# Router computed inside the merge's last products, with the normalisation applied to tokens on partitions

## The reference

```python
def merge_branches(gates, o_a, o_b, w_o_a, w_o_b, w_out):
    g_a, g_b = jnp.split(gates, 2, axis=-1)
    y = jax.nn.sigmoid(g_a) * (o_a @ w_o_a) + jax.nn.sigmoid(g_b) * (o_b @ w_o_b)
    return y @ w_out

def hier_moe(h, router_grp, router_grp_b, router_exp, router_exp_b, w_gate, w_up, w_down):
    t = h.reshape(-1, shape[-1])
    grp_p = jax.nn.softmax((t @ router_grp + router_grp_b).astype(jnp.float32), axis=-1)
    p_grp, g_sel = lax.top_k(grp_p, 1)                       # one of 4 groups
    exp_logits = (t @ router_exp + router_exp_b)...reshape(-1, N_GROUPS, EXPERTS_PER_GROUP)
    in_grp = jnp.take_along_axis(exp_logits, g_sel[:, :, None], axis=1)[:, 0]
    top_logit, top_idx = lax.top_k(in_grp, TOP_K)            # two of its 8 experts
    w_top = jax.nn.softmax(top_logit, axis=-1) * p_grp
    ...
        hid = silu(einsum('td,edf->tef', t, w_gate[grp])) * einsum('td,edf->tef', t, w_up[grp])
        out = out + einsum('tef,efd->td', hid * combine[:, grp, :, None], w_down[grp])

    h_lat = h_lat + m_lat[2] * y_lat
    h_lat = h_lat + m_lat[5] * hier_moe(
        modulate(rmsnorm(h_lat, norm_ffn_g[l]), m_lat[3], m_lat[4]), ...)
```

## Time and profile before

| | |
|---|---|
| median of 3 runs | 2619.45 us |
| profiled execution, its own time | 2621.55 us |
| its span | 2619.7 us |
| TensorE matmul busy | 2470.2 us (94%) |
| DVE busy | 1424.4 us (54%) |
| ACT busy | 1186.0 us (45%) |
| mean granted TensorE clock | 0.970 |
| chain that ended last, by engine | PE 75%, DVE 8%, issue 5%, DMA 5%, ACT 4% |

### The profile page before, as it was taken

The page is one execution under the profiler, slowest core; times in us unless marked ns, Lnnn a source line. Parts: engine busy times, 40 slices in busy tenths (PEclk is TensorE's granted clock), DMA queues, the critical chain, the costliest instruction groups (busy, mean ns, idle before and its releaser), DMA issues.

```text
span 2619.7 us, 52357 instructions
## 1 busy us (share of the span) xinstructions
PE 2470.2 (94%) x23199; PEld 2135.1 (82%) x23199; DVE 1424.4 (54%) x2229; ACT 1186.0 (45%) x1707; POOL 306.8 (12%) x425
## 2 busy tenths in 40 slices
PE   6999999999999999999999989899888889799998
PEld 6999888799999998878899965785477778678786
DVE  4654545466546645443666456445245540278885
ACT  4434466444444444564444355321254421167773
POOL 0100000021101100000311000641133321000000
PEclk8999999999999999999999989889899899899999
DMA  6754522256656644322566411101100004379993
GB/s 217 246 192 167 192 97 104 81 195 233 216 178 213 230 164 171 129 97 101 173 237 222 154 66 46 54 15 57 65 4 4 4 27 141 96 240 365 365 365 126
DMA packets 268884, 396.07 MB, mean 151 GB/s; under 512 B 9320, under 2 KB 172829, under 8 KB 268525
## 3 DMA queue, kind: packets, MB, share of 16 engines
q1 hardware_dynamic: 266921, 389.25, 43.4%
q0 software_dynamic: 1120, 2.17, 0.3%
q10 hardware_dynamic: 612, 1.24, 0.1%
HBM read 391.59 MB, written 1.05 MB: 150 GB/s over the span
## 4 chain that ended last, share of the span: by engine, by line
PE 75%; DVE 8%; issue 5%; DMA 5%; ACT 4%; POOL 2%; SPq 0%; ACTq 0%; DVEq 0%; POOLq 0%
PE ps L282 74%; DMA RB<-in_moe_w_up 5%; DVE gwl L431 2%; POOL H L1415 2%; ACT gwh L422 1%; POOL AR L2535 0%; ACT wh L422 0%; PE ps L1093 0%; DVE wl L431 0%; PE ps L520 0%; DVE AR L1677 0%; ACT AR L2752 0%; DMA RB<-in_ffn_w_gu 0%; ACT AR L2744 0%; DVE AT L1178 0%
## 5 line engine op out<-in xcount | busy, mean ns | idle before, releaser
L431 DVE TENSOR_TENSOR wl<-RB,wh 128x2048 fp32r<-128x2048 f32 (+4 forms) x188 | 412.5, 2197 | 294.5 <-ACT wh L422 293.9
L282 PE MATMUL ps<-H,RB 128*128 128x256 f32 (+1 forms) x1712 | 455.5, 423 | 1.1 <-ACT H L1515 1.1
L422 ACT ACTIVATE wh<-RB 128x2048 fp32r<-128x2048 f32 (+4 forms) x188 | 342.3, 1825 | 236.7 <-PE ps L282 205.3
L282 PEld LDWEIGHTS ps<-H,RB 128*128 128x128 f32 x1712 | 325.5, 193 | 115.1 <-issue 77.4
L282 PE MATMUL ps<-xhf,wl 128*128 128x256 f32 x1408 | 404.4, 287 | 14.0 <-DVE xlf L651 9.3
L282 PE MATMUL ps<-xlf,wh 128*128 128x256 f32 x1408 | 401.0, 285 | 0.0
L282 PE MATMUL ps<-xhf,wh 128*128 128x256 f32 x1408 | 400.8, 285 | 0.0
L282 PE MATMUL ps<-AR 64*64 64x64 f32 (+4 forms) x8296 | 276.1, 242 | 47.2 <-issue 19.7
L282 PEld LDWEIGHTS ps<-AR 64*64 64x64 f32 (+2 forms) x8296 | 241.9, 148 | 80.3 <-issue 51.0
L282 PEld LDWEIGHTS ps<-xhf,wl 128*128 128x128 f32 x1408 | 273.0, 194 | 24.9 <-DVE wl L431 14.8
L282 PEld LDWEIGHTS ps<-xlf,wh 128*128 128x128 f32 x1408 | 273.0, 194 | 0.1
(11 more groups left out here) (425 smaller groups left out, 4155.0 us busy)
## 6 DMA issues: line engine op xcount, KB each, us to landing
RB<-in_ffn_w_gu SPq DMA_DIRECT2D x88, 1024.0 KB, 7.7
RB<-in_w_in SPq DMA_DIRECT2D x25, 2048.0 KB, 7.7
RB<-in_ffn_w_down SPq DMA_DIRECT2D x16, 2048.0 KB, 7.8
RB<-in_w_gate SPq DMA_DIRECT2D x16, 2048.0 KB, 8.2
RB<-in_moe_w_gate SPq DMA_DIRECT2D x32, 1024.0 KB, 7.7
RB<-in_moe_w_up SPq DMA_DIRECT2D x32, 1024.0 KB, 10.2
RB<-in_moe_w_down SPq DMA_DIRECT2D x32, 1024.0 KB, 8.2
RB<-in_ada_w SPq DMA_DIRECT2D x12, 2048.0 KB, 9.9
```

The source lines that it names most:

```text
L282: return M.matmul(o, lhsT, rhs, start=start, stop=stop, skip_group_check=True)
L422: S.activation(self.pair(h)[0], of(slot_of(*key)), ACT.Copy).then_inc(*did("high", *mark))
L431: V.tensor_tensor(lo, of(slot_of(*key)), hi.bitcast(F32), ALU.subtract).then_inc(*did("low", *mark))
```

## The change

- The router's weights RTW are multiplied once by (1 + scale) of each feature, and the product of the shift with the unscaled RTW is added to the router's bias RTB. The 8 matmuls for that ("shifted") stand at the start of `merge` on TensorE; two small DVE instructions follow (L3004 and L3005 of the changed kernel).
- A new class `Route` holds the work on x. `Route.pe(c)` is issued behind the out2 product c + 1 and takes raw XT[c]: two transposes, two matmuls for the logits, and two matmuls that sum the squares (ACT, L3159) with tokens on partitions, so that the norm is one number per partition (1/rms, `rs`). The transposed rows get it as a scale when ACT copies them out, the logits in one DVE instruction each.
- The first two halves of expert weights are split within out2 (ACT behind tile 3 and 5, DVE the same); half 2 is split among the gathering as before.
- The group is chosen from the logits, by a scan, without the exponential. The `ranks` matmuls, the places, CHOSEN and the flag come directly behind it; the experts' choice and weights run on DVE while TensorE gathers.
- The gathering and its split are ahead of the branch. Scale and shift are applied to the gathered tokens: ACT writes X1 with scale and bias (L3204) and then copies it to xh (L3207); DVE subtracts from X1.
- out2 uses three PSUM banks, the logits bank 3, the transposed rows banks 4 to 7. The norm into HA is made in `dense` only.

```diff
@@ merge: tensor()
+                ps = bank(("shifted",), ("rt_bias",))
+                for k in range(KD):
+                    ins = mm(ps[:, 0:36], MOD[:, 24 + k, 0:1].broadcast_to([128, 128]), RTW[:, k, :], k == 0, k == KD - 1)
+                ins.then_inc(*did("shifted"))
                 branch_pe(0, OAT)
...
-                    ps = bank(("out2", c), ("mixed2", c))
+                    ps = bank(("out2", c), ("mixed2", c), among=(0, 1, 2))
...
+                    if c:
+                        route.pe(c - 1)
+                route.pe(KD - 1)
...
+            def pe(self, c):
+                if c == 0:
+                    self.ps = bank(("route",), ("logits", 1), among=(3,))
+                    PE.wait_ge(*at("rt_w"))
+                PE.wait_ge(*at("mixed2", c))
+                for t in LAT:
...
+                    ins = M.transpose(ps[:, 128 * (c % 4):128 * (c % 4) + 128], XT[:, c, 128 * t:128 * t + 128], ident)
...
+                for t in LAT:
+                    mm(self.ps[:, 36 * t:36 * t + 36], XT[:, c, 128 * t:128 * t + 128], RTW[:, c, :], c + t == 0, False)
+                PE.wait_ge(*at("squared", "n3", c))
+                for t in LAT:
+                    ins = mm(self.ps[:, 72 + 2 * t:74 + 2 * t], self.XS[:, c, 128 * t:128 * t + 128], ones[:, 0:2], False,
+                             c == KD - 1)
...
+            def act(self):
+                S.activation(self.ms, EPS, ACT.Sqrt).then_inc(*did("spread_root"))
                 for c in range(KD):
...
+                    AC.wait_ge(*at("mixed2", c))
+                    S.activation(self.XS[:, c, :], XT[:, c, :], ACT.Square).then_inc(*did("squared", "n3", c))
+                    if c in (3, 5):
+                        self.ws_g.high(c // 2)
...
+            def places_pe(self):
+                PE.wait_ge(*at("grouped"))
...
+                PE.wait_ge(*at("chosen"))
+                for k in range(KD):
...
+            def places_act(self):
...
+                    S.activation(self.X1[k % 2], ps_of("xm", k), ACT.Identity, bias=MOD[:, 24 + k, 0:1],
+                                 scale=SCL[:, 2, k:k + 1]).then_inc(*did("xm_out", k))
+                    AC.wait_ge(*at("xm_out", k))
+                    S.activation(self.xh[:, k, :], self.X1[k % 2], ACT.Copy).then_inc(*did("xm_high", k))
...
+        def experts(route):
+            route.places_pe()
+            route.places_act()
+            route.places_dve()
             for x in (PE, DV, AC, PO, SP):
                 x.wait_ge(*at("known"))
...
@@ gathered: tensor()
-                PE.wait_ge(*at("chosen"))
...
+                PE.wait_ge(*at("combined"))
                 ps = bank(("cw",), ("cw_out",), among=work)
```

More of the change, by code:

```diff
@@ new lines, in places_dve @@
+                ps = ps_of("ranks")
+                V.scalar_tensor_tensor(out=rank, in0=ps[:, 0:8].rearrange("p (t g) -> p t g", t=2), scalar=1.0, in1=sel,
+                                       op0=ALU.add, op1=ALU.mult).then_inc(*did("v"))
+                V.tensor_reduce(flag[:, 0:1], ps[:, 8:12], AXX, ALU.max).then_inc(*did("v"))
+                DV.wait_ge(*upto("v"))
+                V.tensor_scalar(rank, rank, -1.0, None, ALU.add).then_inc(*did("rank"))
+                V.tensor_scalar(flag[:, 1:2], flag[:, 0:1], 128.0, None, ALU.is_le).then_inc(*did("v"))
@@ new lines, in places_dve @@
+                DV.wait_ge(*at("rank"))
+                for t in range(2):
+                    for g in range(4):
+                        ins = V.tensor_scalar(self.CHOSEN[:, t, g, :], cst(C_NUM), rank[:, t, g:g + 1], None, ALU.is_equal)
+                ins.then_inc(*did("chosen"))
+                DV.wait_ge(*upto("v"))
+                V.tensor_copy(self.FLAG, flag[:, 1:2]).then_inc(*did("known"))
+                V.tensor_reduce(xg, px.rearrange("p t g e -> p t e g"), AXX, ALU.add).then_inc(*did("v"))
@@ L3335, in scalar @@
             def scalar():
-                ws.high(1)
-                for k in range(KD):
-                    AC.wait_ge(*at("xm", k))
-                    S.activation(xh[:, k, :], ps_of("xm", k), ACT.Copy).then_inc(*did("xm_high", k))
-                    if k in (1, 4):
-                        ws.high(2 if k == 1 else 3)
                 for g in (0, 2):
@@ L3460, in scalar @@
             def scalar():
+                squares_act("n3d", XT, HB)
+                root_act("n3d", T, 1.0 / DM, EPS[:, 0:1], RST)
+                for c in range(KD):
+                    AC.wait_ge(*at("unit_x", "n3d", c))
+                    S.activation(HA[:, c, :], HA[:, c, :], ACT.Identity, bias=MOD[:, 24 + c, 0:1],
+                                 scale=SCL[:, 2, c:c + 1]).then_inc(*did("u_a", 2, c))
+                AC.wait_ge(*at("u_a", 2, KD - 1))
                 S.activation(xh[:, :, :], HA, ACT.Copy).then_inc(*did("xd_high"))
@@ L3479, in vector @@
             def vector():
+                squares_dve("n3d", XT, HB)
+                root_dve("n3d", RST)
+                DV.wait_ge(*at("rstd", "n3d"))
+                for c in range(KD):
+                    V.tensor_tensor(HA[:, c, :], XT[:, c, :], RST, ALU.mult).then_inc(*did("unit_x", "n3d", c))
                 DV.wait_ge(*at("turned", "cmb"))
```

278 lines of the change are left out of this document (138 added, 140 removed).

## The result

In the first comparison, four runs each, the changed kernel took 2595.44 us (2594.85 to 2603.60) against 2619.66 (2618.48 to 2623.50): ratio 0.9911, 95% interval 0.9895 to 0.9927. By the medians it is 24.2 us less, by the ratio 23.3. Two later comparisons of the same pair, in other sessions, gave 0.9933 (0.9915 to 0.9951) and 0.9940 (0.9921 to 0.9958): 17.5 and 15.7 us by the ratios, 16.8 and 13.0 by the medians. Most of what follows is about that difference.

A forecast was written before the change was run, and what follows sets the result against it. The chain from out2's end to the first expert product, 52.4 us, set the end; its new terms summed to 35.8, 16.6 less. 2621.55 - 16.6 = 2604.9, less 2.1 to the median: about 2603.0 us, range 2599.5 to 2608.5.

The forecast's parts named there:

- six sets: Router sets between out2 products, ahead of the last product's end: 60 loads at full clock, 7.0 us.
- last two sets and result: Two router sets behind the last out2 product, 20 loads, 2.3 us, and 0.25 us until the result is there.
- VectorE to the group: Reciprocal, two logits, maximum, comparison, two scans and selection on DVE, at 0.2 us each: 1.5 us.
- branch: Branch on TensorE between gathering and cw, hidden by nothing: 0.6 us, taken from ACT's first instruction after the flag.
- branch costs more: Rival: the branch costs TensorE up to 2.4 us, 1.8 above the term, giving 2604.8; 14%.
- Small matmuls do not overlap: Rival: small matmuls alternating with full products cost 0.25 to 0.38 us each instead of 0.117; kernel at 2628; 3%.
- The clock: Clock falls 5.4 us after TensorE stops, where the gathering begins: `ranks` at full clock, gathering keeps its 1.7 us loss.
- the clock stays full: Rival: the clock stays full through the short pauses around `ranks`, 1.7 us more won, 2601.3; 20%.
- Sets between the blocks: Router work between out2 products: one set is 10 loads, 1.17 us on TensorE, and its waits cost nothing.
- Late split chain: Rival: the split chain on ACT and DVE ends too late, some 3.3 us lost, 2606.3; 8%.
- gain given back: Rival: loads, not TensorE, keep the experts' pace, so the gain is lost there; 2614 if two thirds went; 4%.
- early halves: Weight halves 0 and 1 split within out2: may move one x tile by some 0.2 us.

The follow-up runs named there:

- b2: Changed kernel with the branch taken ahead of the gathering again; merge to first expert product 153.7 us.
- a4: Changed kernel with 16 more transposes ahead of the second block's norm; ratio to before 0.9939.
- e3: Changed kernel, unchanged, run once more; 2600.65 us, ratio to before 0.9940.
- b1: Changed kernel with the eight router sets behind out2's blocks instead of between them; merge to first expert product 157.0 us.
- e4: Same edit to the changed kernel as b1, run again; 2598.41 us, ratio to before 0.9938.
- b3: Changed kernel without weight halves split within out2, three split among the gathering instead; merge to first expert product 154.6 us.
- d1: Changed kernel with ScalarE squaring transposed tiles, `shifted` in TensorE's merge waits, early splits ahead of their tiles' squares; merge to first expert product 147.2 us.
- d3: d1 plus filling products in TensorE's two waits of the choice, gathering in fp32r, last split behind it; 2586.83 us, ratio to before 0.9874.

## Why the prediction was wrong

The step that failed is its last: "The profiled execution gives 2621.55 - 16.6 = 2604.9; it lay 2.1 us above the median, so against the median of 2619.45 the forecast is 2603.0". It took a median of three runs as the level of the rest of the kernel, and the range added 1.5 to 2 us for the errors of the edit's terms and nothing for that level. The runs show that the merge begins anywhere from 2134.9 to 2142.1 us in before, and from 2133.8 to 2141.8 in the changed kernel and its variants. The three runs of before were on the high side (later medians 2616.79, 2617.44, 2617.89 and 2613.64), the first runs of the changed kernel on the low side (later 2599.95 and 2600.65). 8.3 of the 26.6 us between the two profiles came from there, and nothing shows that the change had a part in them. Against the later sessions the forecast gain holds: 16.6 us forecast, 17.5 and 15.7 by the ratios, 15.7 by the stretches. That it holds so well is partly luck: the sets and the branch were put too high by 1.3 us, the clock's part too low by 0.4 to 3.6, as the table shows.

By its terms, full clock unless said, first profile after:

| term | forecast | measured |
|---|---|---|
| `shifted` | 1.9 | 1.8 (45.40 - 43.61); 3.5 where the clock fell |
| six sets | 7.0 | 6.6 (4.57 - 3.47 each) |
| last two sets and result | 2.55 | 2.27 (2259.15 to 2261.42) |
| root | 0.25 | 0.29 |
| VectorE to the group | 1.5 | 1.54 (2261.71 to 2263.25) |
| `ranks` | 1.4 | 1.7; 2.2 to 2.3 in the other three profiles |
| places and CHOSEN | 2.2 | 2.2 (2264.97 to 2267.18) |
| gathering, cw, turns | 18.3 | 18.4; 19.3 to 19.6 in the others |
| branch | 0.6 | 0 |
| sum | 35.8 | 34.8; 36 to 38 in the others (52.4 less what their stretch is below 169.4) |

- *Branch*: the turns stand where the gathering's 48 products end, 2284.63, with nothing between, so TensorE's flag load and branch lie beside products already queued. I had charged it in full. In the open it is 0.75 us (b2). TensorE's load of the flag ran at 2277.0, 7.6 us before they ended. The rival "branch costs more" is refuted.
- *Small matmuls do not overlap*: refuted, 1.03 us for ten loads.
- *The clock*: this step had the mechanism wrong too. I took the 5.4 us of the standstill before, counted them from the end of the sums, and so left `ranks` at full clock. The clock fell 1.7 to 2.6 us after the sums: in the middle of `ranks` in the first profile, at or near their start in the other three. That is the 0.9 us that the prediction named and left out, and up to 1.3 us more in the gathering. The prediction also gave `shifted` the full clock, and in a4 and e3 it fell there (1.7 us). The rival "the clock stays full" came in no profile of the changed kernel.
- *Sets between the blocks*: the price was a little high, 1.17 us for what took 1.1. Their place, which the prediction gave no weight and b1's expectation took to be free of effect, matters: behind out2 they cost 3.6 to 3.7 us more (b1, e4).
- *Late split chain, gain given back*: both refuted by the profile after. The early halves, which the prediction charged with up to 0.2 us of harm, are worth 1.3 us (b3).

## What to carry to other kernels

Ask how much the untouched part of the kernel varies before giving an absolute time. Where its clock falls now and then, three runs don't show the scatter, and the range has to hold that scatter beside the errors of the edit. A single pair of profiles can show a gain in code that nobody changed; split the difference by stretches first. In this kernel the small products did better between large ones than behind one another (3.6 to 3.7 us). And a wait that is moved on one engine has to be followed through the splits queued behind it.

## What the runs showed of the hardware

- The granted clock fell to half while TensorE was busy without a pause, after three or four sets of ten small loads (b1: 0.51 in a window with 9.30 of 9.30 us busy; e4 the same); the same sets between blocks of 256-column products ran at 1.00.
- Small loads run at about 0.107 us at full clock (ten in 1.07 us) and at 0.203 at half (ten in 2.03), in b1. In the gathering, at full clock, an fp32 product with 512 columns takes 0.86 us (two loads, each 0.43 us behind the last, in d1 from 2270.43 on) and an fp32r product 0.23 (d3). So a rounded part and its rest (0.46) cost little more than half of one fp32 product where the other factor is zeros and ones.
- Reading the flag and branching, with nothing queued ahead, cost TensorE 0.75 us and VectorE 0.72 (b2). With products queued they cost TensorE nothing that the profile shows: no idle time between 2284.63 and the turns.
- One kernel on one chip scatters by 14 us (2608.28 to 2622.40 in 24 runs). The second block's first transposes began at 1507.3 to 1508.9 us in six profiles, the merge at 2133.8 to 2142.1 in the unshifted ones: the scatter comes from the stretch between them, where TensorE is busy 88% of the time with many short pauses and the granted clock is 0.92 to 0.94.
